# Attention in pairs of heads on row halves, with the probabilities scaled on GpSimd

## The chip, the cores and the metric

One core of a Trainium2 chip runs the whole program. The metric is the device time of one execution in microseconds; before, the median of three runs is 4497.36 us (4497.18 to 4500.56).

## The reference

The reference is a stack of six layers over 512 tokens of width 1024, all float32. The first two layers join two attentions each: A (8 heads, keys chosen by an indexer) and B (8 heads, a band of 128 keys and a sink logit), then C (8 heads; 31 compressed keys, and two causal branches, each with a gate) and D (8 latent heads of 64 + 32 dimensions). Then follow four layers with modulation by a conditioning vector: full attention over 512 tokens and 256 context tokens, attention with a neighbourhood bias (NA), a convolution and a Fourier mixer, each with an MLP. Every attention is a softmax of this kind:

```python
s = jnp.einsum('bqgrd,bnkgd->bngrqk', qb, kb).astype(jnp.float32) * scale
s = jnp.where(mask[None, :, None, None], s, -jnp.inf)
m = jnp.maximum(jnp.max(s, axis=-1, keepdims=True), sink)
p = jnp.exp(s - m)
p = p / (jnp.sum(p, axis=-1, keepdims=True) + jnp.exp(sink - m))
o = jnp.einsum('bngrqk,bnkgd->bnqgrd', p.astype(v.dtype), vb)
```

In C each branch's output is multiplied by its gate and the three are added; masked rows whose keys are all hidden give zero.

## The kernel before, in words

The program is written out by hand for each engine. A list of stages (project, norm, attention, compress, down, fast, rpb, conv and others) is built first, and each engine walks it with a function of the same name. At the end of a stage every engine waits for all others. Within a stage the order on each engine is what its loop emits, and semaphores are the only links.

Weights come through a ring of three slots (RING = 3). SP issues block b when block b - 3 is freed (L998), by PE's last matmul on it or by DVE's last sum. An ada block is a weight block that DVE multiplies by the conditioning vector and sums (L1868, L1872); PE reduces the sums over the partitions with small matmuls (`modulation`, L1064), DVE takes the result and starts on the next block. A block rides on a group of a project stage: `ride(a)` at the end of a group first does the modulation of the block before and then notes this one.

There are five attention stages: A and B together (8 passes), C (12), D (4), GQA (8 passes of 512 queries over 768 keys, then 8 of 256 context queries over 256) and NA (8 passes over 768 keys with a bias). A pass is two heads. Queries and keys of the two heads lie on partitions 0 to 63 and 64 to 127, except in D, where each head has 96 partitions of its own. The work is cut into units of 128 rows. In all but D a unit is 64 queries of both heads: POOL copies the two Q halves into the diagonal blocks of a 128x128 tile (L2318, L2319), whose other blocks are zero, and one matmul multiplies it by the keys of both heads. In D a unit is 128 queries of one head. For a unit u PE does, in this order,

```python
for u in range(U + lag + 4):
    if u < U:
        scores(u)
    if u >= lag + 4:
        weigh((u - lag - 4) // 4, (u - lag) % 4)
    if lag <= u < U + lag:
        turn(u - lag)
```

`scores` (L1283) also adds the mask as a bf16 matmul (L1287); `turn` (L1301) transposes the probabilities tile by tile; `weigh` (L1320) is a quarter of the weighting of four units (a chunk of 256 queries), on column halves, one for each head. DVE adds the bias in NA (L2059), takes the negated maximum (L2063, or L2066 and L2069 with a sink or a clamp), inverts the sum of the exponentials (L2085) and multiplies the probabilities by it and by the gate (L2089, L2091); ACT does the exponential with its sum (L1629) and copies the turned tiles from PSUM (L1612); DVE takes the output (L2101, L2103). Up to 512 keys four units are in flight (PSUM banks 0 to 3, turned tiles in banks 4 and 5, outputs in 6 and 7); at 768 keys there are two (two banks each, turned tiles in 4 and 5 as one). The bias of NA is a table in DRAM that POOL loads for each pass (L2226). f32 matmuls appear in the trace as two records each.

## Time and profile before

| | |
|---|---|
| median of three runs | 4497.36 us |
| profiled execution, its own time | 4497.19 us |
| its span | 4495.3 us |
| PE busy | 4225.3 us (94%) |
| DVE, ACT, POOL busy | 1807.4, 1002.6, 569.6 us |
| granted clock, mean | 0.951 |

The span runs from the first to the last instruction; the time has some 2 us around it. A busy time counts the records of an engine as one piece where they overlap; the ends of matmuls are modelled, and a record's end reaches some 0.17 us over the start of the next. A clock of 1.00 is 2.4 GHz.

### The profile page before, as it was taken

The page shows a single profiled execution, that of the slowest core. Times are in us where ns is not written, and L with a number is a line of the kernel's source. Part 1 is how long each engine was busy: PE and PEld are TensorE (multiplying, and loading weights), DVE is VectorE, ACT ScalarE, POOL GpSimd, SP SyncE. Part 2 cuts the span into 40 slices and gives each one's busy share as a digit, 9 for nine tenths or more (in the row PEclk, how much of TensorE's full clock was granted, in tenths as well). Part 3 has the DMA queues.
Part 4 walks back from the last instruction along what each step waited for, and adds up shares of the span by engine and source line. Part 5 has one row for each costly group of instructions (what it writes and reads, how often), then busy time and mean ns, then how long its engine had stood idle before and what let it go on. Part 6 is the DMA issues. An engine that isn't in the chain of part 4 may idle for free. (4 is left out here: it accounts for less than half of the span.)

```text
span 4495.3 us, 41307 instructions
## 1 busy us (share of the span) xinstructions
PE 4225.3 (94%) x15852; PEld 2623.4 (58%) x15856; DVE 1807.4 (40%) x3067; ACT 1002.6 (22%) x2179; POOL 569.6 (13%) x896
## 2 busy tenths in 40 slices
PE   8998979799999799999989999999999999999998
PEld 3354445244555356665545454888644788747887
DVE  3573347443266022112010384665264565404443
ACT  1150116232156121100010252201122202112020
POOL 0030013010012000000000121111130111101112
PEclk8999969689999799999999999999999999999999
DMA  3113320202000212232111101454210344211221
GB/s 131 60 38 107 120 69 11 76 1 87 26 17 1 54 56 94 94 112 94 56 56 56 51 23 38 143 176 150 75 56 19 119 162 169 80 52 66 88 94 38
DMA packets 206737, 339.16 MB, mean 75 GB/s; under 512 B 19472, under 2 KB 77232, under 8 KB 206512
## 3 DMA queue, kind: packets, MB, share of 16 engines
q1 hardware_dynamic: 188000, 320.42, 20.6%
q10 hardware_dynamic: 17136, 10.07, 0.9%
q0 software_dynamic: 1408, 6.03, 0.5%
q8 instruction: 129, 2.11, 0.2%
q14 instruction: 64, 0.52, 0.0%
HBM read 330.48 MB, written 6.03 MB: 75 GB/s over the span
## 5 line engine op out<-in xcount | busy, mean ns | idle before, releaser
L1096 PE MATMUL psum<-H,ring 128*128 128x512 f32 (+1 forms) x2608 | 1145.4, 599 | 33.5 <-issue 16.8
L1096 PEld LDWEIGHTS psum<-H,ring 128*128 128x128 f32 (+1 forms) x2608 | 494.9, 191 | 665.1 <-issue 651.7
L1224 PE MATMUL psum<-arena,ring 128*128 128x256 f32 x1536 | 343.3, 380 | 2.8 <-ACT arena L1512 2.8
L1283 PE MATMUL psum<-arena,sd 128*128 128x256 f32 (+4 forms) x896 | 311.1, 453 | 13.9 <-POOL sd L2319 10.5
L1872 DVE SCALAR_TENSOR_TENSOR arena<-ring,cond,arena 128x512 f32<-128x512 f32 x448 | 319.0, 750 | 8.0
L1224 PEld LDWEIGHTS psum<-arena,ring 128*128 128x128 f32 x1536 | 290.4, 190 | 44.0 <-ACT arena L1512 5.2
L2252 POOL TENSOR_TENSOR ring<-ring 128x1024 f32<-128x1024 f32 x48 | 162.4, 3383 | 813.1 <-DVE arena L1762 813.1
L1224 PE MATMUL psum<-arena 128*128 128x256 f32 x1152 | 255.5, 379 | 0.0
L2063 DVE TENSOR_REDUCE small<-psum 128x1 f32<-128x768 f32 (+4 forms) x288 | 198.5, 689 | 138.2 <-PE psum L1283 95.7
L1612 ACT ACTIVATE arena<-psum 128x768 f32<-128x768 f32 (+5 forms) x352 | 191.3, 543 | 221.2 <-PE psum L1301 217.8
L1224 PEld LDWEIGHTS psum<-arena 128*128 128x128 f32 x1152 | 218.9, 190 | 29.8
L1855 DVE TENSOR_TENSOR mods<-psum,vec 128x4 f32<-128x4 f32 (+1 forms) x48 | 7.7, 161 | 564.5 <-PE psum L1064 563.6
L1180 PE MATMUL psum<-arena,ring 128*128 128x512 f32 x512 | 225.4, 593 | 0.2 <-issue 0.2
L1629 ACT ACTIVATE arena<-psum,small 128x768 f32<-128x768 f32 (+5 forms) x352 | 219.1, 622 | 22.9 <-DVE small L2063 17.2
L1301 PE MATMUL psum<-ident,arena 128*128 128x128 f32 (+1 forms) x1240 | 210.7, 287 | 7.1 <-ACT arena L1612 3.2
L1096 PE MATMUL psum<-CH,ring 128*128 128x256 f32 x928 | 207.4, 382 | 0.0
L1301 PEld LDWEIGHTS psum<-ident,arena 128*128 128x128 f32 (+1 forms) x1240 | 133.5, 140 | 117.3 <-issue 79.3
L1320 PE MATMUL psum<-arena 128*64 128x256 f32 (+2 forms) x1360 | 192.5, 381 | 8.1 <-ACT arena L1612 7.1
L1283 PEld LDWEIGHTS psum<-arena,sd 128*128 128x128 f32 x896 | 151.0, 198 | 83.4 <-issue 75.1
L1096 PEld LDWEIGHTS psum<-CH,ring 128*128 128x128 f32 x928 | 176.6, 191 | 38.4 <-issue 12.1
L1224 PE MATMUL psum<-H,ring 128*128 128x256 f32 x768 | 183.5, 394 | 7.6 <-ACT H L1552 5.1
L1470 ACT ACTIVATE arena<-psum 128x512 f32<-128x512 f32 (+4 forms) x123 | 66.4, 541 | 549.8 <-PE psum L1096 549.5
(214 smaller groups left out, 4906.7 us busy)
## 6 DMA issues: line engine op xcount, KB each, us to landing
ring<-in_mlp_w SPq DMA_DIRECT2D x64, 2048.0 KB, 7.9
ring<-in_ada_w SPq DMA_DIRECT2D x48, 2048.0 KB, 7.9
ring<-in_na_qkv SPq DMA_DIRECT2D x6, 2048.0 KB, 7.9
ring<-in_pw SPq DMA_DIRECT2D x6, 2048.0 KB, 7.9
ring<-in_ab_in SPq DMA_DIRECT2D x5, 2048.0 KB, 7.8
ring<-in_cd_in SPq DMA_DIRECT2D x4, 2048.0 KB, 7.6
ring<-in_at_qkv SPq DMA_DIRECT2D x3, 2048.0 KB, 7.7
ring<-in_ab_out SPq DMA_DIRECT2D x2, 2048.0 KB, 11.0
```

The source lines that it names most:

```text
L1096: last = nc.tensor.matmul(out, lhs, rhs, start=(k == 0), stop=(k == len(t.pairs) - 1))
L1180: last = nc.tensor.matmul(bank(m), w[:, k, P * m:P * m + P], hid[:, KD * kb + k, :], start=(kb == 0 and k == 0), stop=(kb == 3 and k == KD ...
L1224: last = nc.tensor.matmul(out, w[:, i, P * m:P * m + P], x[:, i, :], start=(opens and m == 0 and i == 0), stop=(i == k - 1), skip_group_ch ...
L1283: last = nc.tensor.matmul(psum[:, buf + c0:buf + c1], q, p["k"](head, a * P + c0, a * P + c1), start=True, stop=not masks)
L1301: last = nc.tensor.transpose(psum[0:w, t0 + j * P:t0 + j * P + P], probs[u % d["nb"]][:, j * P:j * P + w], ident[:, :])
L1320: last = nc.tensor.matmul(psum[HD * g:HD * g + HD, (6 + pr % 2) * BANK + q0:(6 + pr % 2) * BANK + q1], p["v"](g, kt), turned_b[0:p["krows" ...
L1470: nc.scalar.activation(t.dst, src, ACT.Copy).then_inc(act_took, 1)
L1612: nc.scalar.activation(dst, src, ACT.Copy).then_inc(copied, 1)
L1629: nc.scalar.activation(probs[u % d["nb"]][:, 0:nk], psum[:, s0:s0 + nk], ACT.Exp, bias=small[:, c:c + 1], accum_out=small[:, 8 + c:9 + c]) ...
L1872: ins = nc.vector.scalar_tensor_tensor(partial[:, v, :], w[:, k, :], cond[:, k, v:v + 1], partial[:, v, :], ALU.mult, ALU.add)
L2063: nc.vector.tensor_reduce(small[:, c:c + 1], psum[:, s0:s0 + nk], AX, ALU.max, negate=True).then_inc(negmax_ready, 1)
L2252: nc.gpsimd.tensor_tensor(a21, a11, a21, ALU.subtract).then_inc(s3_made, 1)
```

## The change

- A unit becomes a pair: 128 queries of two heads. Each head's scores are a matmul of its own on 64 rows, partitions 0 to 63 or 64 to 127 (`of_head`); the diagonal tile, its copies on POOL and half_select are gone. D keeps 96 rows.
- Two pairs are in flight in every stage. At 768 keys a pair takes three banks, and its second head's columns start with key tiles 4 and 5 so that no matmul crosses a bank. The fourth matmul of a pair waits for the second through half_scored, since the two share a bank. The turned tiles and the outputs share banks 6 and 7, and each waits until what was in the bank is taken. Four tiles of one head are turned and copied at a time; the third group of a pair (tiles 4 and 5 of both heads) is copied by DVE.
- The multiplication by the inverse sum and the gate moves from DVE to POOL.
- The sink, and the clamp of the compressed branch (as a key of -1e29), become one more column of the scores by a matmul with the identity (L1346 of the new program); DVE's and ACT's operations for them go. The compression stage no longer moves the gates.
- NA's bias lies in CX and CH, once for each head, and is loaded for both row halves of a tile: four transfers a pass instead of two.
- An ada block moves: it no longer rides on the group at c0 == 2048 of the first layer's projection, and a group with no weights and this block stands after the second group of the second layer's. All later blocks shift in the ring.
- The sinks are loaded in four parts.

```diff
@@ first layer's projection
-            ab_groups.append((b, ab_tiles(b, c0, c0 + 512), next_ada() if c0 == 2048 else None))
+            ab_groups.append((b, ab_tiles(b, c0, c0 + 512), None))
@@ second layer's projection
             groups_.append((b, (c0, c1), next_ada()))
+            if c0 == 512:
+                groups_.append((None, None, next_ada()))
@@ the order of the pairs
+        def order(st):
+            pairs, chunks = st["pairs"], st["chunks"]
+            for i in range(len(pairs) + 6):
+                if i < len(pairs):
+                    yield "scores", pairs[i], None
+                if 0 <= i - 2 < len(pairs):
+                    for t in pairs[i - 2]["turns"]:
+                        yield "turn", t, pairs[i - 2]
+                if st["wide"]:
+                    if i >= 5 and i % 2 and (i - 5) // 2 < len(chunks):
+                        yield "weigh", chunks[(i - 5) // 2], None
+                elif i >= 4 and (i - 4) // 2 < len(chunks):
+                    yield "weigh", chunks[(i - 4) // 2], i % 2
@@ PE
+                    for b in pair["banks"]:
+                        open_bank(b)
+                    runs = [(0, 0, BANK), (1, BANK, nk), (1, 0, BANK), (0, BANK, nk)] if nk > BANK else [(0, 0, nk), (1, 0, nk)]
+                    for m, (g, k0, k1) in enumerate(runs):
+                        at = off[g] + pair["column"](g, k0 // P)
+                        if m == 3:
+                            n["half"] += 1
+                            pe.wait_ge(half_scored, n["half"])
+                        last = nc.tensor.matmul(psum[:, at:at + k1 - k0], p["q"](g, qt * P, qt * P + P),
+                                                p["k"](g, a * P + k0, a * P + k1), start=(m < 3), stop=not masks,
+                                                skip_group_check=nk > BANK or p["sink"] is not None)
+                        if m == 1 and nk > BANK:
+                            last.then_inc(half_scored, 1)
...
+                        if p["sink"] is not None:
+                            last = nc.tensor.matmul(psum[:, off[g] + nk:off[g] + nk + 1], ident[:, :], p["sink"](g),
+                                                    start=False, stop=True, skip_group_check=True)
...
+                    for b in pair["banks"]:
+                        bank_freed[b] = (exp_done, 2 * pair["id"] + 2)
+                def turn(t, pair):
+                    rows, c0 = min(P, pair["p"]["krows"]), t["bank"] * BANK
+                    pe.wait_ge(probs_ready, 2 * pair["id"] + t["gs"][-1] + 1)
+                    open_bank(t["bank"])
@@ ACT
+                for i in range(len(pairs) + 2):
+                    if st["wide"] and i >= 2:
+                        copies(pairs[i - 2], i - 2)
+                    if i < len(pairs):
+                        exponential(pairs[i], i, 0)
+                        exponential(pairs[i], i, 1)
+                    if not st["wide"] and i >= 2:
+                        copies(pairs[i - 2], i - 2)
@@ DVE
+                for i in range(len(pairs) + 8):
+                    if i < len(pairs):
+                        negmax(pairs[i], 0)
+                        negmax(pairs[i], 1)
+                    if 0 <= i - 1 < len(pairs):
+                        scale(pairs[i - 1], 0)
+                        scale(pairs[i - 1], 1)
+                    if 0 <= i - 2 < len(pairs):
+                        copies(pairs[i - 2], i - 2)
+                    j = i - (5 if st["wide"] else 6)
+                    if j >= 0 and j % 2 == 0 and j // 2 < len(chunks):
+                        take(chunks[j // 2])
@@ POOL
-                        nc.gpsimd.tensor_copy(q_diagonal[0:HD, u % Q_BUFS, 0:HD], q[0:HD]).then_inc(pool_steps, 1)
-                        nc.gpsimd.tensor_copy(q_diagonal[HD:P, u % Q_BUFS, HD:P], q[HD:P]).then_inc(q_ready, 1)
+                            pool.wait_ge(inverse_ready, u + 1)
+                            pb, by = pair["probs"][g][:, 0:nk], small[:, 24 + c:25 + c]
+                            if p["gate"] is not None:
+                                nc.gpsimd.tensor_scalar(pb, pb, by, p["gate"](pair["qt"], g), ALU.mult,
+                                                        ALU.mult).then_inc(probs_ready, 1)
+                            else:
+                                nc.gpsimd.tensor_scalar(pb, pb, by, None, ALU.mult).then_inc(probs_ready, 1)
```

The order of the instructions in two places. PE in the GQA stage at 768 keys, before (L1301 transposes, L1283 scores, L1320 weighting; two units):

```order
L1301 MATMUL psum<-ident,arena 128x128 x6
L1283 MATMUL psum<-arena,sd 128x512
L1283 MATMUL psum<-arena,sd 128x256
L1320 MATMUL psum<-arena 64x256 x2
L1301 MATMUL psum<-ident,arena 128x128 x6
L1283 MATMUL psum<-arena,sd 128x512
L1283 MATMUL psum<-arena,sd 128x256
L1320 MATMUL psum<-arena 64x256 x4
```

and in the change (L1335 scores, L1360 transposes, L1381 weighting; two pairs):

```order
L1335 MATMUL psum<-arena 128x512
L1335 MATMUL psum<-arena 128x256
L1335 MATMUL psum<-arena 128x512
L1335 MATMUL psum<-arena 128x256
L1360 MATMUL psum<-ident,arena 128x128 x12
L1335 MATMUL psum<-arena 128x512
L1335 MATMUL psum<-arena 128x256
L1335 MATMUL psum<-arena 128x512
L1335 MATMUL psum<-arena 128x256
L1360 MATMUL psum<-ident,arena 128x128 x12
L1381 MATMUL psum<-arena 64x256 x12
```

The weighting of a chunk stood in quarters between scores and transposes and now stands in one piece behind the transposes of every second pair. PE in the second layer's projection, before (L1096 a group of 32 matmuls, L1064 a modulation):

```order
L1096 MATMUL psum<-H,ring 128x512 x32
L1064 MATMUL psum<-ones,arena 128x1 x8
L1096 MATMUL psum<-H,ring 128x512 x32
L1064 MATMUL psum<-ones,arena 128x1 x8
L1096 MATMUL psum<-H,ring 128x512 x32
```

and in the change (L1155 a group, L1123 a modulation):

```order
L1155 MATMUL psum<-H,ring 128x512 x32
L1123 MATMUL psum<-ones,arena 128x1 x8
L1155 MATMUL psum<-H,ring 128x512 x32
L1123 MATMUL psum<-ones,arena 128x1 x16
L1155 MATMUL psum<-H,ring 128x512 x32
```

Two modulations stand behind one another after the second group; the one after the first output block of the first layer is gone.

## Rows read from the trace of the kernel before

**Rows 1.** Attention stages: window, length, PE, PEld, DVE, ACT, POOL busy, clock, DMA
```profile
251.00:339.00 88.00, 83.17 (x556) 49.41 (x560) 70.06 (x264) 61.98 (x226) 31.32 (x127) 1.00 0.13 48
666.00:781.00 115.00, 110.36 (x700) 64.84 (x702) 90.79 (x355) 77.59 (x288) 47.21 (x189) 0.94 0.01 1
932.00:980.00 48.00, 45.79 (x262) 25.68 (x264) 33.00 (x100) 31.95 (x98) 0.00 (x0) 0.92 0.00 1
1236.00:1465.00 229.00, 224.14 (x1217) 123.10 (x1216) 141.29 (x304) 135.47 (x289) 42.87 (x185) 1.00 0.03 9
2538.00:2732.00 194.00, 189.46 (x1024) 106.95 (x1024) 153.62 (x263) 108.66 (x192) 35.61 (x138) 0.98 0.10 26
```

**Rows 2.** Timeline at 768 keys: start, us, engine, line, operation, count [idle before]
```profile
1300.62 0.87 PE L1301 MATMUL psum<-ident,arena 128*128 128x128 f32 x6
...
1301.33 1.46 PE L1283 MATMUL psum<-arena,sd 128*128 128x512 f32 x4
1301.53 0.81 ACT L1612 ACTIVATE arena<-psum 128x768 f32<-128x768 f32 x1 [0.99 <-PE psum L1301]
...
1302.72 1.08 PE L1320 MATMUL psum<-arena 128*64 128x256 f32 x8
1302.83 0.96 DVE L2063 TENSOR_REDUCE small<-psum 128x1 f32<-128x768 f32 x1 [0.40 <-PE psum L1283]
...
1303.70 0.15 DVE L2085 RECIPROCAL small<-small 128x1 f32<-128x1 f32 x1
...
1303.74 0.87 PE L1301 MATMUL psum<-ident,arena 128*128 128x128 f32 x6
...
1306.42 0.87 PE L1301 MATMUL psum<-ident,arena 128*128 128x128 f32 x6
```

**Rows 3.** Timeline of the context passes, 256 keys
```profile
1440.99 0.44 PE L1301 MATMUL psum<-ident,arena 128*128 128x128 f32 x2
...
1443.57 0.44 PE L1301 MATMUL psum<-ident,arena 128*128 128x128 f32 x2
```

**Rows 4.** Timeline of the last attention, 768 keys with a bias
```profile
2621.85 0.70 DVE L2059 TENSOR_TENSOR psum<-psum,CX 128x512 f32<-128x512 f32 x1 [0.70 <-PE psum L1283]
...
2622.33 0.87 PE L1301 MATMUL psum<-ident,arena 128*128 128x128 f32 x6
2622.59 0.96 DVE L2063 TENSOR_REDUCE small<-psum 128x1 f32<-128x768 f32 x1
...
2628.12 0.87 PE L1301 MATMUL psum<-ident,arena 128*128 128x128 f32 x6
```

**Rows 5.** Timeline of PE at the indexer's matmuls on row halves
```profile
115.11 1.13 PE L1158 MATMUL psum<-arena 64*128 64x512 f32 x4
116.17 1.04 PE L1121 MATMUL psum<-arena 128*22 128x512 f32 x2
```

**Rows 6.** POOL's groups by line and shape: count, busy us, mean ns, idle before
```profile
L2318 POOL COPY sd<-arena 64x64 f32<-64x64 f32 x320 | 75.5, 236 | 395.1 <-PE psum L1283 301.2 <-PE psum L1287 86.2 <-remote 4.5
...
L2269 POOL TENSOR_TENSOR arena<-arena 128x512 f32<-128x512 f32 x24 | 30.5, 1269 | 70.2 <-DVE arena L1825 70.2
...
L2269 POOL TENSOR_TENSOR arena<-arena 128x256 f32<-128x256 f32 x24 | 17.4, 723 | 120.1 <-DVE arena L1825 120.1
```

**Rows 7.** Timelines of PE and DVE in the second layer's projection
```profile
412.95 29.86 PE L1096 MATMUL psum<-H,ring 128*128 128x512 f32 x64 [0.93 <-DVE H L1964]
...
471.91 1.84 PE L1064 MATMUL psum<-ones,arena 128*128 128x1 f32 x16
473.61 27.71 PE L1096 MATMUL psum<-H,ring 128*128 128x512 f32 x64
...
474.67 9.36 DVE L1872 SCALAR_TENSOR_TENSOR arena<-ring,cond,arena 128x512 f32<-128x512 f32 x14
```

**Rows 8.** Group of ACT's copies of 512 turned columns
```profile
L1612 ACT ACTIVATE arena<-psum 128x512 f32<-128x512 f32 x32 | 19.1, 597 | 7.1 <-PE psum L1301 6.9
```

**Rows 9.** Transfers of the page: count, KB each, us to landing
```profile
ring<-in_cd_in SPq DMA_DIRECT2D x4, 2048.0 KB, 7.6
```

More of the change, by code:

```diff
@@ new lines, in weigh @@
+                def weigh(chunk, half):
+                    p, c0, parts, n_parts = chunk["p"], chunk["c0"], chunk["parts"], len(chunk["parts"])
+                    if half != 1:
+                        pe.wait_ge(act_copied, chunk["copied"][0])
+                        if chunk["copied"][1]:
+                            pe.wait_ge(dve_copied, chunk["copied"][1])
+                        if st["wide"] or (p["first"] and c0 == 0):
+                            open_bank(chunk["bank"])
+                    starts = st["wide"] or (c0 == 0 and p["first"])
+                    ends = st["wide"] or p["last"]
+                    split = n_parts if half is None else n_parts // 4 * 2
+                    for i in range(split if half == 1 else 0, n_parts if half == 1 else split):
@@ L1325, in weigh @@
-                    if quarter == 3:
-                        last.then_inc(pv_done, 1)
-                        if p["last"] and j + 4 == p["units"]:
-                            pairs[0] += 1
-                U, lag = len(units), d["turn"]
-                for u in range(U + lag + 4):
-                    if u < U:
-                        scores(u)
-                    if u >= lag + 4:
-                        weigh((u - lag - 4) // 4, (u - lag) % 4)
-                    if lag <= u < U + lag:
-                        turn(u - lag)
@@ L1338, in attention @@
-                n["unit"] += U
-                n["pair"] += pairs[0]
+                            psum[HD * g:HD * g + HD, at + q0:at + q1], p["v"](g, kt),
+                            chunk["turned"][0:p["krows"], kt, g, q0 - c0:q1 - c0], start=(i < 2 and starts),
+                            stop=(i >= n_parts - 2 and ends), skip_group_check=True)
+                    if half != 0:
+                        last.then_inc(pv_done, 1)
+                        if chunk["takes"]:
+                            bank_freed[chunk["bank"]] = (o_taken, chunk["taken"])
@@ L1341, in compress @@
+                for kind, x, y in order(st):
+                    if kind == "scores":
+                        scores(x)
+                    elif kind == "turn":
+                        turn(x, y)
+                    else:
+                        weigh(x, y)
             def compress(st):
@@ L1369, in compress @@
                     last.then_inc(misc_pe, 1)
[L1370 to L1376 removed]
+                n["misc"] += 6
             def latnorm(st):
@@ L1631, in attention, with exponential @@
-                n["unit"] += U
-                n["pv"] += U // 4
-                act.wait_ge(copied, n["unit"])
+                pairs = st["pairs"]
+                def exponential(pair, i, g):
+                    p, nk, off = pair["p"], pair["nk"], pair["off"][g]
+                    u = 2 * pair["id"] + g
+                    c = u % 8
+                    act.wait_ge(negmax_ready, 2 * pair["id"] + 2 if nk > BANK else u + 1)
+                    if i >= 2:
+                        before = [t["seq"] for t in pairs[i - 2]["turns"] if g in t["gs"]]
+                        act.wait_ge(turned, before[-1])
+                    more = p["sink"] is not None
+                    nc.scalar.activation(pair["probs"][g][:, 0:nk + more], psum[:, off:off + nk + more], ACT.Exp,
+                                         bias=small[:, c:c + 1], accum_out=small[:, 8 + c:9 + c]).then_inc(exp_done, 1)
@@ L1635, in compress @@
+                act.wait_ge(act_copied, pairs[-1]["copied"][0])
             def compress(st):
@@ L2122, in compress @@
+                dve.wait_ge(o_taken, chunks[-1]["taken"])
             def compress(st):
```

451 lines of the change are left out of this document (189 added, 262 removed).

## The prediction

> **What bounds the kernel now.** I read the page first (one core, PE busy 94% of the span, clock 0.951), then asked for the busy time of each engine in the five attention stages [rows 1]. See two things there: the stages last 88, 115, 48, 229 and 194 us, 674 of 4495 us in all, and PE is busy in 94 to 98% of each, while DVE stands at 62 to 80%, ACT at 56 to 70% and POOL at 41% at most. So PE's own list of instructions sets these stages, and the question is what the change leaves on that list and what it makes PE wait for. The timeline of the 768-key stage [rows 2] gives prices. Six transposes start at 1300.62 and the scores at 1301.33; the scores (512 and 256 keys, two records each) take the 1.39 us to 1302.72; units follow each other after 3.12 and 2.68 us in turn, and differ by four passes of the weighting, so one pass is 0.107 us. Two units (128 queries of two heads) take 5.80 us. Streaming is 1.29 + 0.64 + 0.64 = 2.57 us a unit, so changing between the three kinds of matmul costs 0.33 us a unit.
>
> **1. Row halves for the scores.** Before, a block-diagonal Q multiplies 128 rows; after, each head multiplies on its own 64 rows. The work in keys is the same (two heads by 128 queries, nk keys each), so this pays only if the two halves run at once. The trace has such a pair: the indexer's 64-row matmuls of two heads [rows 5] start together, and 512 keys of both take 1.06 us until the next matmul, with four passes. One after another they would be 4 x 0.433 = 1.73 us (64 passes of 512 columns take 27.71 us [rows 7]); at once 2 x 0.433 plus 0.2 of fixed cost is 1.07. I take full overlap: 1.39 us for a pair of heads at 768 keys instead of 2.78. The third matmul of a pair (keys 0 to 511 of the second head) has a bank of its own; the fourth waits for the second (the counter half_scored), whose data are long there when the first ends.
>
> **2. The 768-key steps.** PE's list per pair is now scores 1.39, transposes 12 x 0.107 and a half of 24 weighting passes: 3.96 us plus changes, against 5.80. It will not get there. The turned tiles and the weighted sums share banks 6 and 7, so the third group of transposes waits until ACT has copied the first: handover 0.27 (1301.26 to 1301.53 [rows 2]), copy of 512 columns 0.60 [rows 8], 0.2 back to PE (my allowance for a semaphore to PE, here and below): 1.07 us after the first group, where it could start after 0.43. The weighting waits for the second copy, 0.5 later. With 0.15 to change to transposes (1303.58 to 1303.74), even steps: 1.39 + 0.15 + 0.43 + 1.07 + 0.43 = 3.47; odd steps 1.39 + 0.15 + 0.43 + 0.27 + 1.10 + 0.20 + 2.65 = 6.19; floor 9.66 us for two pairs (11.60 before).
> The second limit is the new hop. The order is fixed: scores of the next pair, then both maxima on DVE, then the reciprocals of this pair, two multiplications on POOL, this pair's transposes, copy, weighting. Around two steps: 1.39 + 0.21 (1302.62 to 1302.83) + 0.87 + 0.96 for two maxima [rows 2] + 0.15 + 2p + 0.20 + 0.43 + 0.27 + 0.60 + 0.20 + 2.65 = 7.93 + 2p, with p the time of one 128x768 multiplication on POOL. In the last attention each maximum has a bias addition ahead of it, 0.74 from start to start [rows 4], so 9.41 + 2p.
>
> **The price p.** POOL has no such operation in this trace. The nearest from below is its one-input copy, 0.236 for 64 elements; from above its two-input multiplication, 1.269 for 512 and 0.723 for 256 [rows 6], that is 0.18 fixed and 2.13 ns an element. With the same fixed part the copy gives 0.8 ns an element: p between 0.80 and 1.82. The operation reads one tensor and two scalars, so I stay near the copy: p = 0.95. Then two pairs take 9.83 in the first 768-key stage and 11.31 in the last, against 11.60.
> The Trainium skill (GPSIMD Engine Reference, Engine selection) says that one-input work on GpSimd is "roughly line-rate"; by that p would be 0.8 and the total 4428. The same page (Elementwise, side-by-side cycle accounting) gives 1.8 cycles an element as the best case of a tight loop; by that p would be near 1.3 and the total 4462. No row here shows either.
>
> **3. The sum.**
> - GQA stage, 32 pairs at 768 keys: 16 x (11.60 - 9.83) = -28. Its 16 context pairs take 2.58 each now [rows 3]; scores halve (-0.43) and a set of changes goes; with POOL in the loop I take -0.5 each, -8. Together -36.
> - NA stage: 16 x (11.60 - 11.31) = -5, and +1 for the first bias, which DVE already waits for, since it is now eight transfers instead of four: -4.
> - A and B (88 us): 256 keys save 0.43, so 4 x 1280 keys save 8.5 and 4 x 896 save 6.0; a set of changes fewer, 32 x 0.25 = 8; the sink is now a matmul by the identity, four passes a pair at the 0.106 of the ada block's small matmuls (16 in 1.70 us [rows 7]), 16 x 0.43 = 6.8 back. That is -16; the loop of two pairs will not keep all of it: -12.
> - C (115 us): 8 x 1280 keys, 17; changes 12; the same extra column for the 31-key passes, +7: -20, as above with a little held back.
> - D (48 us): 96 rows, no halves; fewer changes (-4), later probabilities (+1.5): -2.5.
> - The moved ada block. It leaves the end of the first projection, where DVE's sums lie under PE's value tiles, and comes as a group of its own without weights after the second group of the second layer. PE there does the modulation matmuls twice in a row, and the second needs the DVE sums of the block before, which start only after the first. Where one block rides now, the group ends at 471.91, the modulation takes 1.70 and DVE's sums end at 484.03, 12.1 after the group [rows 7]; with 0.2 and another modulation the next weights start 14.0 us after the group's end instead of 1.7, +12.3, less 1.7 for the one no longer done after the first output block: +10.6. The clock follows: behind the wait for the norm the 64 passes of 412.95 took 29.86 us, those of 473.61 27.71 [rows 7], +2.2. The next weights also find their ring slot free only at the group's end; the 7.6 us of loading [rows 9] lie under the DVE sums. In all +13.
> - Inputs: three more small transfers ahead of the first weights, +1; the gate matmuls and copy of the compression gone, -1. POOL's copies of Q, 320 for each half [rows 6], go at no gain: it idled and PE seldom waited for them.
> Sum: -36 - 4 - 12 - 20 - 2.5 + 13 = -61.5. Against the profiled execution's 4497.2 (median 4497.4) this is **4436 us**.
>
> **The rivals.**
> *Halves in lock step* (0.14). In-order starts could make the four matmuls of a pair run as two rounds of 512 columns: 1.72 us instead of 1.29. The equal pair of rows 5 can't tell. PE's floor becomes 10.52 for two pairs, and the NA loop 11.74: 11 us and 7 us less gain, 4454.
> *A loop price in between* (0.19), p = 1.3: each loop grows by 0.7 for two pairs, 11 us in each 768-key stage, and a little in the others: about 4462.
> *POOL at the two-input rate, slower than before* (0.10), p = 1.82. The GQA period is 11.57, so the stage keeps only its context gain (-5); NA's is 13.05, +23 +1; POOL also delays the short stages, where I leave -5, -12 and +1; with +13 for the ada block the sum is +16: 4513. It decides from p = 1.1 on in NA alone (9.41 + 2p = 11.6) and from about 1.7 on for the whole. For it: two-input multiplications are the only arithmetic POOL does here, at that rate. Against it: the copy.
> *It pays for itself only* (0.05): the pairs are not in flight as described, since banks or buffers are held longer than the order shows, PE waits away what the halves save, and the time stays within 9 us.
> A lower clock I hold for unlikely: PE would stream 70% of the time in NA and its gaps stay near 1 us; it held full clock at two gaps per 2.9 us.
>
> **How the numbers follow.** A difference under 0.2% (9 us) could not be told from none. Forecast 0.52, lock step 0.14, middle price 0.19: faster 0.85; same 0.05; slower 0.10. The range takes p = 0.80 (4428, and up to 20 below for the short stages keeping all and the ada stall being half) and reaches above over both faster rivals together (4480): 4405 to 4480.
>
> **What would show it.** POOL's TENSOR_SCALAR at 128x768 near 0.95 us; two score rows of a pair starting together, 1.4 us per pair; PE waiting for ACT copies and for POOL in transposes; PE idle of about 12 us once after the second group of the second layer, for DVE; stages of about 76, 95, 45, 193 and 190 us. A POOL row over 1.7 us, or scores of 2.8 us, would make the forecast wrong.

## The result, and the profile after

The changed kernel takes 4628.85 us (median of four runs, 4627.25 to 4635.16), the kernel before 4498.48 on the same chip: a ratio of 1.0293, 95% interval 1.0277 to 1.0309. It is 130 us **slower**, where 61 us faster was forecast, and outside the range. The profiled execution of the changed kernel took 4627.25 us (span 4625.5, mean granted clock 0.932; before 0.951).

The busy time in the five attention stages of the changed kernel, as [rows 1] show it before (window, length, PE, PEld, DVE, ACT, POOL busy, clock, DMA; each window runs from the first score matmul to just behind the last weighting matmul):

```profile
249.40:341.90 92.50, 78.86 (x624) 47.27 (x624) 34.12 (x136) 52.69 (x170) 60.73 (x64) 1.00 0.07 24
681.50:795.00 113.50, 105.20 (x768) 60.99 (x768) 41.34 (x196) 72.82 (x258) 50.19 (x96) 0.93 0.01 2
946.20:1006.00 59.80, 50.05 (x272) 29.58 (x272) 18.47 (x68) 30.43 (x90) 34.16 (x32) 0.90 0.00 1
1260.00:1523.00 263.00, 209.40 (x1216) 129.05 (x1216) 109.69 (x248) 121.86 (x274) 168.84 (x96) 0.90 0.04 11
2592.00:2857.00 265.00, 193.30 (x1024) 120.42 (x1024) 133.30 (x240) 98.23 (x194) 156.70 (x96) 0.81 0.15 38
```

Windows cut in this way are 87.4, 115.9, 48.4, 228.9 and 195.0 us long before, so the stages together went from 675.6 to 793.8 us. That is 118 of the 130 us, and 104 of them are in the two 768-key stages (the fourth and fifth rows). There PE is no longer busy all the time (80% and 73%, before 98% and 97%), and its clock is 0.90 and 0.81 instead of 1.00 and 0.98. No engine took PE's place: POOL is busy for 64% and 59%.

POOL's groups for the new multiplication (line, operation, shapes, count, busy us, mean ns, idle before):

```profile
L2352 POOL TENSOR_SCALAR arena<-arena,small 128x768 f32<-128x768 f32 x112 | 245.3, 2203 | 198.0 <-DVE small L2108 197.9
...
L2352 POOL TENSOR_SCALAR arena<-arena,small 128x512 f32<-128x512 f32 x16 | 24.8, 1563 | 0.0
...
L2352 POOL TENSOR_SCALAR arena<-arena,small 128x128 f32<-128x128 f32 x24 | 14.2, 601 | 34.0 <-DVE small L2108 33.9
L2349 POOL TENSOR_SCALAR arena<-arena,small 128x512 f32<-128x512 f32 x16 | 12.2, 770 | 1.9 <-DVE small L2108 1.9
...
L2349 POOL TENSOR_SCALAR arena<-arena,small 128x128 f32<-128x128 f32 x16 | 7.0, 448 | 9.8 <-DVE small L2108 9.8
```

L2352 multiplies by one scalar column, L2349 by two (the inverse sum and the gate). One operation costs 2.50 ns an element ((2203 - 601) / 640) and 0.28 us fixed; two operations in one instruction cost a third of that, 0.84 ns an element. The time of one 128x768 multiplication, the prediction's p, was 2.20 us, above its upper bound of 1.82.

Two rows of the list of PE's waits (us in total, times, longest), and PE's, POOL's and the weight loads' (PEld) timelines over two pairs of the first 768-key stage, which [rows 2] show before (sd_rstd is one of the tiles that hold probabilities; the last row of PE's timeline is cut by the end of the window asked for):

```profile
PE psum L1360 <- POOL arena L2352: 95.9, 96, 2.0
...
PE psum L1360 <- POOL sd_rstd L2352: 21.6, 15, 1.5
```

```profile
1329.86 1.89 PE L1335 MATMUL psum<-arena 64*128 64x512 f32 x8
1331.69 1.09 PE L1360 MATMUL psum<-ident,arena 128*128 128x128 f32 x8
...
1333.68 1.89 PE L1335 MATMUL psum<-arena 64*128 64x512 f32 x8
1336.04 0.66 PE L1360 MATMUL psum<-ident,arena 128*128 128x128 f32 x4 [0.47 <-POOL arena L2352]
1338.22 1.74 PE L1360 MATMUL psum<-ident,arena 128*128 128x128 f32 x8 [1.52 <-POOL arena L2352]
1339.89 3.79 PE L1381 MATMUL psum<-arena 128*64 128x256 f32 x24
1343.61 0.70 PE L1335 MATMUL psum<-arena 64*128 64x512 f32 x3
```

```profile
1333.78 8.74 POOL L2352 TENSOR_SCALAR arena<-arena,small 128x768 f32<-128x768 f32 x4 [5.01 <-DVE small L2108]
```

```profile
1329.86 0.73 PEld L1335 LDWEIGHTS psum<-arena 64*128 64x128 f32 x6 [0.39 <-issue]
1331.06 0.29 PEld L1335 LDWEIGHTS psum<-arena 64*128 64x128 f32 x2 [0.47 <-PE psum L1335]
```

Two stretches of the same two pairs in the columns of the stages above; the granted clock stands behind POOL's busy time:

```profile
1338.22:1339.89 1.67, 1.67 (x8) 1.34 (x8) 0.00 (x0) 0.60 (x1) 1.67 (x1) 0.58 0.00 0
1339.89:1341.50 1.61, 1.61 (x9) 1.01 (x10) 0.69 (x1) 1.44 (x3) 1.61 (x2) 0.50 0.00 0
```

See four things. The period of two pairs is 13.75 us (1329.86 to 1343.61), 11.60 before. The transposes of the odd pair wait for POOL, head by head. The scores of a pair take 1.83 us (1329.86 to 1331.69), not 1.39, and the weight loads of the fourth matmul wait for L1335, another matmul of the same pair: that is the counter half_scored. And behind the waits for POOL (0.47 and 1.52 us) the weighting's 24 passes take 3.72 us (1339.89 to 1343.61), where 2.57 was reckoned: the granted clock was 0.58 in the transposes just ahead of them and 0.50, the lower of its two levels (1.2 GHz), in the first 1.61 us of them.

### The profile page after: what moved, and what is told of

It reads as the page before. It is cut to its first block and busy times, and to the rows that moved or that the text cites. A ratio compares the mean times of both kernels' runs of the same rounds, so it can differ in the third digit from the quotient of the medians.

```text
span 4625.5 us, 40970 instructions
## 1 busy us (share of the span) xinstructions
PE 4214.6 (91%) x15976; PEld 2643.9 (57%) x15976; DVE 1655.2 (36%) x2668; ACT 957.0 (21%) x2062; POOL 875.9 (19%) x616
## 5 line engine op out<-in xcount | busy, mean ns | idle before, releaser
L1155 PE MATMUL psum<-H,ring 128*128 128x512 f32 (+1 forms) x2608 | 1151.5, 601 | 33.0 <-issue 16.6
L1155 PEld LDWEIGHTS psum<-H,ring 128*128 128x128 f32 (+1 forms) x2608 | 497.4, 192 | 669.0 <-issue 656.2
L2352 POOL TENSOR_SCALAR arena<-arena,small 128x768 f32<-128x768 f32 (+3 forms) x240 | 369.1, 1552 | 287.1 <-DVE small L2108 286.9
L1283 PE MATMUL psum<-arena,ring 128*128 128x256 f32 x1536 | 343.3, 380 | 2.8 <-ACT arena L1563 2.8
L1283 PEld LDWEIGHTS psum<-arena,ring 128*128 128x128 f32 x1536 | 290.4, 190 | 44.0 <-ACT arena L1563 5.2
L1360 PE MATMUL psum<-ident,arena 128*128 128x128 f32 (+1 forms) x1144 | 197.9, 304 | 114.4 <-POOL arena L2352 95.9
L2098 DVE TENSOR_REDUCE small<-psum 128x1 f32<-128x768 f32 (+7 forms) x352 | 204.0, 614 | 226.6 <-PE psum L1342 110.8
L1283 PE MATMUL psum<-arena 128*128 128x256 f32 x1152 | 255.5, 379 | 0.0
L1335 PE MATMUL psum<-arena 64*128 64x512 f32 (+4 forms) x960 | 220.2, 501 | 21.4 <-ACT arena L1654 17.0
L1283 PEld LDWEIGHTS psum<-arena 128*128 128x128 f32 x1152 | 218.9, 190 | 29.8
L1654 ACT ACTIVATE arena<-psum,small 128x768 f32<-128x768 f32 (+7 forms) x336 | 204.4, 613 | 151.5 <-DVE small L2098 90.7
L1360 PEld LDWEIGHTS psum<-ident,arena 128*128 128x128 f32 (+1 forms) x1144 | 135.3, 152 | 169.9 <-POOL arena L2352 127.9
L1155 PE MATMUL psum<-CH,ring 128*128 128x256 f32 x928 | 207.6, 382 | 0.0
L2329 POOL TENSOR_TENSOR arena<-arena 128x512 f32<-128x512 f32 (+2 forms) x46 | 56.5, 1234 | 770.4 <-DVE arena L2031 763.6
L1155 PEld LDWEIGHTS psum<-CH,ring 128*128 128x128 f32 x928 | 176.7, 191 | 38.3 <-issue 12.0
L1666 ACT ACTIVATE arena<-psum 128x512 f32<-128x512 f32 (+3 forms) x272 | 144.2, 553 | 249.5 <-PE psum L1360 249.1
L1381 PE MATMUL psum<-arena 128*64 128x256 f32 (+2 forms) x1360 | 193.9, 426 | 1.9 <-ACT arena L1666 1.7
L1283 PE MATMUL psum<-H,ring 128*128 128x256 f32 x768 | 182.5, 393 | 7.6 <-ACT H L1603 5.1
```

Source lines behind the costliest of these rows:

```text
L1155: last = nc.tensor.matmul(out, lhs, rhs, start=(k == 0), stop=(k == len(t.pairs) - 1))
L1283: last = nc.tensor.matmul(out, w[:, i, P * m:P * m + P], x[:, i, :], start=(opens and m == 0 and i == 0), stop=(i == k - 1), skip_group_ch ...
L1335: last = nc.tensor.matmul(psum[:, at:at + k1 - k0], p["q"](g, qt * P, qt * P + P), p["k"](g, a * P + k0, a * P + k1), start=(m < 3), stop= ...
L1360: last = nc.tensor.transpose(psum[0:rows, c0:c0 + P], pair["probs"][g][:, k0:k0 + rows], ident[:, :])
L1381: last = nc.tensor.matmul(psum[HD * g:HD * g + HD, at + q0:at + q1], p["v"](g, kt), chunk["turned"][0:p["krows"], kt, g, q0 - c0:q1 - c0], ...
L1654: nc.scalar.activation(pair["probs"][g][:, 0:nk + more], psum[:, off:off + nk + more], ACT.Exp, bias=small[:, c:c + 1], accum_out=small[:, ...
```

## The experiments

Twelve kernels were run, all of them the changed kernel with edits. The ratios are to the kernel before, whose median was 4497.3 to 4498.2 us beside them. A difference between two changed versions is the difference of their medians.

**The price.** A second scalar makes POOL run the form of L2349.

```diff
-                                nc.gpsimd.tensor_scalar(pb, pb, by, None, ALU.mult).then_inc(probs_ready, 1)
+                                nc.gpsimd.tensor_scalar(pb, pb, by, ones[:, :], ALU.mult,
+                                                        ALU.mult).then_inc(probs_ready, 1)
```

> The changed kernel with one edit: the multiplication without a gate gets a second scalar, a column of ones, so that POOL runs the form which takes two scalars. Theory (the price is that of the one-scalar form, not of the operation): a 128x768 multiplication falls from 2.20 us to about 0.99 (the gated ones took 0.34 us + 0.84 ns an element), two pairs at 768 keys from 13.7 us to 10.3 to 10.8, the last attention from about 13.8 to 11.8, and the time from 4629 to 4460 to 4530 us. Rival (POOL is slow at this because it shares its way to the tiles with VectorE, or because of the length): the multiplication stays above 2 us and the time above 4600.

Measured: 4481.15 us, ratio to before 0.9963 [0.9948, 0.9978], that is 148 us less than the changed kernel by one operand and one operation more. POOL's groups, then PE's timeline over two pairs:

```profile
L2352 POOL TENSOR_SCALAR arena<-arena,small,ones 128x768 f32<-128x768 f32 x112 | 109.0, 981 | 237.1 <-DVE small L2108 237.0
...
L2352 POOL TENSOR_SCALAR arena<-arena,small,ones 128x512 f32<-128x512 f32 x16 | 12.1, 768 | 0.1
```

```profile
1289.84 1.89 PE L1335 MATMUL psum<-arena 64*128 64x512 f32 x8
1291.67 1.09 PE L1360 MATMUL psum<-ident,arena 128*128 128x128 f32 x8
...
1297.47 2.81 PE L1381 MATMUL psum<-arena 128*64 128x256 f32 x24
1300.21 1.89 PE L1335 MATMUL psum<-arena 64*128 64x512 f32 x8
```

The period is 10.37 us, no wait for POOL is left in the pairs of 768 keys, and the weighting takes 2.74 us again. The stage's context pairs of 256 keys keep eight waits for POOL, 7.5 us together. So the loss is the price of the form, and the lower clock came with the waits. The time lies in the range that was expected (4460 to 4530), and the rival of a price that stays is out. Three of its stages (the gated one and the two at 768 keys), in the windows' columns as above; the other two last 80.7 and 50.2 us:

```profile
...
669.50:783.20 113.70, 105.30 (x768) 61.08 (x768) 41.41 (x196) 72.91 (x258) 50.19 (x96) 0.93 0.01 2
...
1233.70:1440.00 206.30, 184.90 (x1217) 114.83 (x1218) 109.72 (x248) 120.54 (x274) 79.60 (x96) 0.99 0.05 14
2508.40:2708.00 199.60, 160.66 (x1024) 104.39 (x1024) 131.70 (x240) 98.11 (x194) 78.78 (x96) 0.96 0.20 51
```

**Which form is dear.** The second scalar as a constant:

```diff
-                                nc.gpsimd.tensor_scalar(pb, pb, by, None, ALU.mult).then_inc(probs_ready, 1)
+                                nc.gpsimd.tensor_scalar(pb, pb, by, 1.0, ALU.mult, ALU.mult).then_inc(probs_ready, 1)
```

> The multiplication without a gate as one scalar column and a second multiplication by the constant 1.0. Theory (the dear form is the one with a single operation): 128x768 near 0.98 us, as with the column of ones. Rival (the cheap form needs two scalar columns): 2.2 us and a time near 4629.

Measured once: 4485.69 us, and the multiplication a little cheaper still. One execution can't rank it against the column of ones (4481.15).

```profile
L2352 POOL TENSOR_SCALAR arena<-arena,small 128x768 f32<-128x768 f32 x112 | 100.1, 904 | 243.7 <-DVE small L2108 243.3
```

A price list. This kernel leaves out the division by the sum in the passes without a gate:

```diff
-                                nc.gpsimd.tensor_scalar(pb, pb, by, None, ALU.mult).then_inc(probs_ready, 1)
+                                if g == 0:
+                                    nc.gpsimd.tensor_scalar(pb, pb, 1.0, None, ALU.mult).then_inc(probs_ready, 1)
+                                else:
+                                    nc.gpsimd.tensor_copy(pb, pb).then_inc(probs_ready, 1)
```

> Only a price list: the changed kernel where the multiplication without a gate is left out, and in its place POOL multiplies the first head by the constant 1.0 (one operation, no scalar column) and copies the second head onto itself. It leaves the division by the sum out of those passes. Theory (one operation alone is the dear form, whatever the scalar is): first head near 2.1 us at 128x768, the copy near the 0.8 that was the lower bound of the forecast. Rival (the dear form is one operation by a column): first head 0.9 or less, time below 4490.

```profile
L2353 POOL TENSOR_SCALAR arena<-arena 128x768 f32<-128x768 f32 x64 | 136.4, 2131 | 215.7 <-DVE small L2108 215.6
...
L2355 POOL COPY arena<-arena 128x768 f32<-128x768 f32 x48 | 39.6, 825 | 0.0
```

A single operation is dear with a constant too; the scalar column is not the reason. The copy takes 0.825 us, so the lower bound of 0.80 was close for a copy, and the operation as it was written was simply not of that kind. One execution took 4519.66 us.

**Does the price add along the loop?** The second scalar for the second head of a pair alone:

```diff
-                                nc.gpsimd.tensor_scalar(pb, pb, by, None, ALU.mult).then_inc(probs_ready, 1)
+                                nc.gpsimd.tensor_scalar(pb, pb, by, None if g == 0 else ones[:, :], ALU.mult,
+                                                        *(() if g == 0 else (ALU.mult,))).then_inc(probs_ready, 1)
```

> The changed kernel with the second scalar for the second head of a pair alone: one multiplication at 2.20 us, one at 0.98. Theory (price adds along the loop): 7.93 + 0.43 + 3.2 = 11.55 us for two pairs in the first 768-key stage, plus a little clock, 13.0 in the last; time 4525 to 4555, between 4629 and 4481. Rival (only the slower of the two counts): above 4590.

Measured: 4540.43 us, ratio 1.0093 [1.0078, 1.0108], between the two versions. PE's timeline:

```profile
1296.21 1.89 PE L1335 MATMUL psum<-arena 64*128 64x512 f32 x8
1298.56 0.66 PE L1360 MATMUL psum<-ident,arena 128*128 128x128 f32 x4 [0.46 <-POOL arena L2352]
1299.53 1.09 PE L1360 MATMUL psum<-ident,arena 128*128 128x128 f32 x8 [0.31 <-POOL arena L2352]
1300.96 2.81 PE L1381 MATMUL psum<-arena 128*64 128x256 f32 x24 [0.34 <-ACT arena L1666]
...
1307.52 1.89 PE L1335 MATMUL psum<-arena 64*128 64x512 f32 x8
```

Two pairs take 11.31 us (1296.21 to 1307.52), 11.55 expected. So both heads' prices count, and the rival (only the slower of the two, above 4590 us) is out.

**Is it the loop?** Here the dear form stays. At 768 keys (`wide`) the reciprocals, which release POOL, move between the two maxima of the next pair:

```diff
                     if i < len(pairs):
                         negmax(pairs[i], 0)
-                        negmax(pairs[i], 1)
+                        if not st["wide"]:
+                            negmax(pairs[i], 1)
                     if 0 <= i - 1 < len(pairs):
                         scale(pairs[i - 1], 0)
                         scale(pairs[i - 1], 1)
+                    if i < len(pairs) and st["wide"]:
+                        negmax(pairs[i], 1)
```

> The changed kernel itself, with its dear one-scalar form; only the reciprocals go between the two maxima of the next pair at 768 keys. Theory (the loop of two pairs through VectorE and POOL sets the period, its terms add): 0.9 us less for two pairs in the first 768-key stage and 1.6 us in the last, 40 us in all: 4590. Rival (POOL's own throughput or PE's clock sets it): 4620 to 4629.

Measured: 4569.53 us, ratio 1.0157 [1.014, 1.0174], 59 us less than the changed kernel at an unchanged price of POOL.

```profile
1297.99 1.89 PE L1335 MATMUL psum<-arena 64*128 64x512 f32 x8
...
1305.48 1.09 PE L1360 MATMUL psum<-ident,arena 128*128 128x128 f32 x8 [1.20 <-POOL arena L2355]
1306.91 2.81 PE L1381 MATMUL psum<-arena 128*64 128x256 f32 x24 [0.34 <-ACT arena L1666]
1309.65 1.68 PE L1335 MATMUL psum<-arena 64*128 64x512 f32 x7
```

The period fell by 2.1 us (13.75 to 11.66), more than the 0.9 that the move takes out of the loop. Of the rest 0.98 is the weighting, back from 3.72 to 2.74 us (1306.91 to 1309.65), and 0.24 the eight transposes ahead of it, from 1.67 to 1.43 (1305.48 to 1306.91): less wait also gave the clock back (0.98 in this stage, 0.90 in the changed kernel). So the loop sets the period, not POOL's throughput, which is the same in both. The 59 us are more than the 40 expected, which counted no clock.

**The multiplication elsewhere.** Back on VectorE behind the reciprocals, pairs kept; POOL's loop over the heads is empty:

```diff
-                    nc.vector.reciprocal(small[:, 24 + c:25 + c], small[:, 8 + c:9 + c]).then_inc(inverse_ready, 1)
+                    last = nc.vector.reciprocal(small[:, 24 + c:25 + c], small[:, 8 + c:9 + c])
...
+                        nc.vector.tensor_scalar(pb, pb, by, None, ALU.mult).then_inc(probs_ready, 1)
...
-                        for g in range(2):
+                        for g in ():
```

> The changed kernel with the multiplications back on VectorE behind the reciprocals, pairs and order kept. Theory (the wait for POOL is the loss, the pairs are a gain): 0.62 us a multiplication at 768 keys as before, period of two pairs near PE's floor with halves in lock step, 10.0 to 10.5 us, time 4450 to 4510, at most 20 us from the two-scalar version. Rival (the pairs themselves lose: banks held too long, or VectorE becomes the bound): above 4560.

Measured: 4472.30 us, ratio 0.9942 [0.9927, 0.9957], 9 us less than the two-scalar version, with the same periods: 10.37 us, and 11.57 in the last attention. So the pairs themselves are a gain, and the rival that they lose (above 4560) is out. Then one head on each engine (two scalars on POOL, a counter of its own for VectorE's heads):

```diff
-                    pe.wait_ge(probs_ready, 2 * pair["id"] + t["gs"][-1] + 1)
+                    for g in t["gs"]:
+                        pe.wait_ge((probs_ready, probs_dve)[g], pair["id"] + 1)
```

> Two-scalar form on POOL for the first head of a pair, VectorE multiplies the second head, so the two lie beside each other. The loop of two pairs becomes 7.93 + 0.43 + 1.0 = 9.4 us, below PE's own list, so both 768-key stages go to the floor of PE (10.1 to 10.5 us): 5 to 25 us less than the two-scalar version. Rival (the loop does not bound once the price is small): equal to it within 3 us.

Measured: 4473.68 us, ratio 0.9946 [0.9931, 0.9961]: 7 us less, which is the lower end of what was expected. The last attention did not move (11.56): POOL's half grew dearer beside VectorE's, and PE waits 1.12 us for it in every two pairs there. POOL's and VectorE's timelines in the first 768-key stage:

```profile
1294.59 1.39 POOL L2364 TENSOR_SCALAR arena<-arena,small,ones 128x768 f32<-128x768 f32 x1 [5.17 <-DVE small L2109]
```

```profile
1294.59 0.62 DVE L2120 TENSOR_SCALAR arena<-arena,small 128x768 f32<-128x768 f32 x1
```

**The ada block.**

```diff
-            ab_groups.append((b, ab_tiles(b, c0, c0 + 512), None))
+            ab_groups.append((b, ab_tiles(b, c0, c0 + 512), next_ada() if c0 == 2048 else None))
...
-            if c0 == 512:
-                groups_.append((None, None, next_ada()))
```

> Two-scalar version, and the moved ada block put back to the last output block of the first projection. Theory: 13 to 15 us less than the two-scalar version (two stalls of DVE sums less, one modulation more). Rival (the stall only moves, or the block costs as much in its old place): within 3 us of it.

Measured: 4468.81 us, ratio 0.9935 [0.9918, 0.9951], 12.3 us less than the two-scalar version (13 to 15 expected). PE's timeline of the changed kernel shows where they were (before: the 1.84 at 471.91 of [rows 7]):

```profile
474.14 1.84 PE L1123 MATMUL psum<-ones,arena 128*128 128x1 f32 x16
486.32 3.58 PE L1123 MATMUL psum<-ones,arena 128*128 128x1 f32 x16 [10.33 <-DVE arena L1909]
489.75 30.52 PE L1155 MATMUL psum<-H,ring 128*128 128x512 f32 x64
```

From the group's end to the next weights it is 15.6 us (474.14 to 489.75; 14.0 was reckoned), and the 64 passes behind take 2.8 us longer than the 27.71 of [rows 7]. With the one modulation that is saved elsewhere this is more than 12.3, so the block is not free in its old place either; how much it costs there was not taken apart.

**The halves.** In the gated stage of the two-scalar version both heads at 512 keys take 1.06 us until the next matmul (2 x 0.43 and 0.2 of fixed time), so two matmuls of equal length overlap fully:

```profile
694.03 1.13 PE L1335 MATMUL psum<-arena 64*128 64x512 f32 x4
695.09 0.29 PE L1342 MATMUL psum<-diagm,identb 128*128 128x128 bf16 x2
```

At 768 keys a 512 stands beside a 256. Two scalars, and six matmuls of 256 keys:

```diff
-                    runs = [(0, 0, BANK), (1, BANK, nk), (1, 0, BANK), (0, BANK, nk)] if nk > BANK else [(0, 0, nk), (1, 0, nk)]
+                    runs = [(0, 0, 256), (1, BANK, nk), (0, 256, BANK), (1, 0, 256), (0, BANK, nk),
+                            (1, 256, BANK)] if nk > BANK else [(0, 0, nk), (1, 0, nk)]
...
-                        if m == 3:
+                        if m == 4:
```

> Two-scalar version, and the scores of a pair at 768 keys cut into six matmuls of 256 keys, head by head in turn, so that the halves always hold equal lengths. In the two-scalar version 256, 384 and 512 keys of both heads take 0.64, 0.85 and 1.07 us (full overlap and 0.21 fixed), 768 keys in unequal lengths 1.83. Theory (only unequal neighbours keep the halves in step): 3 x 0.427 + 0.2 = 1.5 us a pair, two pairs 10.37 to 9.7 us in the first 768-key stage and 11.57 to 10.9 in the last, 22 us less than the two-scalar version. Rival (weight loads of the halves come one after another, 12 loads of 0.186 us): 2.0 us or more a pair, and 5 to 20 us slower than it.

Measured: 4464.38 us, ratio 0.9927 [0.991, 0.9943], 17 us less than the two-scalar version. PE's timeline and that of the weight loads:

```profile
1286.11 1.57 PE L1336 MATMUL psum<-arena 64*128 64x256 f32 x12
1287.61 1.09 PE L1361 MATMUL psum<-ident,arena 128*128 128x128 f32 x8
```

```profile
1286.11 1.16 PEld L1336 LDWEIGHTS psum<-arena 64*128 64x128 f32 x12 [0.39 <-issue]
```

The same keys now take 1.50 us (1286.11 to 1287.61), so the rival (12 loads one after another, 2.0 us) is out. But the edit changes two things, the lengths and the place of the wait on half_scored, which now stands ahead of the fifth matmul. The loads say which one the time went to. In the changed kernel the six loads of the first three matmuls are through 0.73 us after the pair's start (1329.86), and the two of the fourth begin only at 1331.06, 1.20 us after it, released by the second matmul (0.47 before in PEld's row). Here the twelve loads have no such gap. The unequal lengths themselves overlap: in the two-scalar version, whose pairs also take 1.83 us, two records of 512 columns start together 0.54 us after a pair's start (1289.84), the first matmul's second one and the third matmul's first (one short stretch; count, ns, first and last start):

```profile
L1335 PE MATMUL psum<-arena x2: 589/589/589, 1290.4 to 1290.4; 64*128 64x512 f32 x2
```

By the lengths the first head's half is free 0.96 us after the start (2 x 0.43 and 0.1, half of the fixed time, to start; an estimate), so the wait costs 0.24 us; with 0.1 to start again that turns 1.50 into 1.84, against 1.83 measured. It is released only after the first matmul's data are through too, though the second is half as long. No run has the unequal lengths without this wait, so the division of the 0.33 us rests on these rows.

In the last attention only 0.3 of the 0.66 us for two pairs came through (period 11.25): there PE waits for POOL that much longer (1.06 and 0.32 us, before 0.72 and 0.31).

**The last attention's loop.** Two scalars, and the reciprocals between the maxima by the same edit as above:

> Two-scalar version; on VectorE at 768 keys the reciprocals of a pair go between the two maxima of the next pair instead of behind both, so POOL starts one maximum (with its bias addition: 1.6 us) earlier. Theory (in the last attention the loop through VectorE's maxima and POOL sets the period, in the first 768-key stage PE's own list does): last attention 11.57 to about 10.4 us for two pairs, first stage unchanged at 10.37; 15 to 20 us less than the two-scalar version. Rival (VectorE's maxima or ACT's exponentials bound the last attention): within 3 us of it.

Measured: 4475.36 us, ratio 0.9947 [0.9933, 0.9962], 6 us less than the two-scalar version, where 15 to 20 were expected; its own four runs spread over 11 us (4470 to 4481). PE's timeline of the last attention:

```profile
2578.94 0.60 PE L1360 MATMUL psum<-ident,sd_rstd 128*128 128x128 f32 x4
2580.69 0.41 PE L1360 MATMUL psum<-ident,arena 128*128 128x128 f32 x2 [1.15 <-ACT arena L1666]
```

POOL is in time now, and ACT is late next: it runs the next pair's two exponentials (2578.18 to 2579.95) ahead of the copies. The period is 11.19 us, from 11.57, where 10.4 was expected: the theory missed the size, and the rival (under 3 us, VectorE or ACT the bound) had named ACT but not the gain.

**Together.** Two scalars, equal halves, reciprocals between the maxima, ada block back:

> Two scalars, equal halves, reciprocals between the maxima, and the ada block put back. If the three gains add: 4481 - 22 - 18 - 12 = 4429 us; if the loop binds again once PE's list is shorter, 4430 to 4445.

Measured: 4450.69 us, ratio 0.9887 [0.987, 0.9903], with runs from 4438 to 4453. Both expectations missed (4429 if the gains add, else 4430 to 4445): together the parts give 30 us over the two-scalar version, one by one 17, 6 and 12. Then with the constant 1.0 as second factor, and VectorE multiplying in the stages of at most 512 keys:

> All three edits of e8 with the constant 1.0 as second factor, and in the attentions of at most 512 keys the multiplications back on VectorE. Theory: the short stages lose PE's waits for POOL (5 us) and the clock falls less often in the gated one (up to 9 us): 4430 to 4445 us against 4451. Rival (POOL's waits cost nothing there, VectorE's extra work does): 4450 to 4460.

Measured: 4440.49 us, ratio 0.987 [0.9855, 0.9885]: 57 us under the kernel before, 188 under the changed one, and inside what was expected (4430 to 4445). The 10 us to the version before are of two edits at once and less than that one's own spread of 15, so neither edit's share is shown. Two pairs take 9.72 us in the first 768-key stage.

```profile
1300.35 1.57 PE L1334 MATMUL psum<-arena 64*128 64x256 f32 x12
...
1310.07 1.13 PE L1334 MATMUL psum<-arena 64*128 64x256 f32 x8
```

## Why the prediction was wrong

**The price p** is the step that failed. The prediction took 0.95 us because "the operation reads one tensor and two scalars"; L2352, the line that sets both 768-key stages, takes one scalar and one operation, and that form took 2.20. The two-scalar form takes 0.98, so 0.95 was the price of another line. The upper bound failed with it: the two-input multiplication at 2.13 ns an element was taken for the dearest thing POOL does, and the one-operation form takes 2.50. POOL had never run that form in the trace, and a bound from other operations needs a reason that it holds.
The Trainium skill (GPSIMD Engine Reference, Elementwise, side-by-side cycle accounting) reckons 512 elements of its best loop at 768 ns; the two-scalar rows agree (768 and 770 ns), the one-scalar row does not (1563). Its "roughly line-rate" for one input (Engine selection) held for the copy (825 ns at 768) and not for the one-operation multiplication.

**The loop** was right. With 0.43 more for the scores, 7.93 + 0.43 + 2 x 2.20 = 12.76 us, and 0.98 of slower weighting and 0.24 of slower transposes make 13.98, against 13.75 measured: its terms are some 0.2 too large together. In the last attention 9.41 + 0.43 + 4.40 = 14.24, against 15.11 (two pairs at 2701.00) at a clock of 0.81 in the stage; with two scalars 11.80 reckoned, 11.57 measured. The earlier reciprocals and the single dear head confirm it from both sides. The rival "POOL at the two-input rate, slower than before" had the mechanism and the sign; its 4513 was too low since p passed even its price, and since it counted no loss of clock and no dearer scores.

**A lower clock I hold for unlikely** was wrong: with two waits for POOL in every two pairs (0.47 and 1.52 us, in the last attention 1.93 and 1.52) the stages stood at 0.90 and 0.81; without these waits, or with a single one of 1.20, the first of them was at 0.99 and 0.98. It cost about 20 us in the first 768-key stage (1.22, the slower weighting and transposes, in each of 16 periods).

**Row halves.** Two equal matmuls overlap fully (1.06 us for 512 keys). At 768 keys a pair took 1.83 us instead of 1.39, and the step that failed is "the fourth waits for the second (the counter half_scored), whose data are long there when the first ends": the fourth's loads were held until 1.20 us after the pair's start. The rival of the lock step, at 0.14, came near that size (1.72, and some 0.1 for changing), but by luck: it wants two rounds of 512 columns, and the third matmul starts 0.54 us after the first, beside the first's second half, where a first round would take 0.86. The six equal matmuls, where nothing waits, bring 1.50; the 0.11 over 1.39 is the rest of the fixed time (the prediction had 0.2 in its 1.07 for 512 keys, and 0.1 in its 1.39).
The Trainium skill (TensorEngine Tiling (Array Packing), Key Properties) says that tiles operate independently; the 1.06 us for two matmuls of 512 keys agrees, and the 1.83 beside 1.50 for the same keys shows that a wait from one tile to the other takes some of it back.

**The sum, term by term** (forecast; changed kernel; two-scalar version, in us against before, stages by their windows): first 768-key stage -36; +34; -23. Last attention -4; +70; +5. A and B -12; +5; -7. C -20; -2; -2. D -2.5; +11; +2. The ada block +13, measured 12.3. In the two-scalar version the price was the forecast's own, and 16 us of the 61 were left (its terms here add to 13). So even at the forecast's price three quarters of the gain are missing:

- The first 768-key stage, 13 us: 16 x 0.54 = 9 by the periods 10.37 and 9.83, which are the dearer scores; 2 in the context pairs, which save 0.37 us each instead of 0.5 with POOL in their loop; 2 not taken apart.
- The last attention, 9 us: 4 by the period (11.57 for 11.31), and the first bias, put at +1. It is there 12.5 us after the last matmul of the projection ahead, 9.6 before, so +2.9. The window shows more, since it starts at the first score: PE waited 4.38 us for POOL's copies of Q there, and waits 0.80 now. These 3.6 us are also the difference between 13 and 16.
- The short stages, 18 us in C, 5 in A and B, 4 in D. The 0.2 us of fixed time of every score pair, seen in [rows 5], was left out: at 128 keys a pair takes 0.42 us, two units took 2 x 0.22, so nothing is saved. Over the 32 masked pairs of A and B, and as many in C, this is about 7 us each. In C 5 us more are PE's waits for POOL's gated multiplication. D has no halves. How the rest of C's and D's expected gain divides between sinks, changes of kind and waits was not taken apart.

## What to carry to other kernels

Price an operation by a row with the same opcode and the same number of operations and scalars in it; if the trace has none, time that form by itself before building a pipeline on it. On POOL, write a one-scalar multiplication with a second factor of 1.0 (tried here in f32, with 128 to 768 elements in a row). When a new engine is put between two others, add its time to the loop of buffers and maxima that closes over it, count the clock that PE loses while it waits, and look for what is queued in front of the next instruction once that wait is gone. A counter between two matmuls is a wait like any other: the timeline of the weight loads shows it where PE's own timeline shows no gap.

## What the runs showed that was not expected

- POOL's tensor-scalar multiplication of 128x768: one operation 2203 ns (2131 with a constant), two operations 981 (904 with the second factor a constant). More work in the instruction takes less than half the time.
- POOL and VectorE multiplying at once: POOL's 0.98 us became 1.39 while VectorE's stayed at 0.62; both started at 1294.59. The Trainium skill (SBUF — State Buffer, Who interferes with whom) says that the two share a port pair, that some modes of VectorE, which `tensor_scalar` can enter, use it, and that whoever issues first then has it for the whole instruction. The 0.41 us more on POOL, within VectorE's 0.62, are compatible with that; which mode VectorE ran in, no run shows.
- The wait on half_scored was released only 1.20 us after a pair's start, though the second matmul, which it waits for, is half as long as the first: the signal of the shorter matmul came after the longer one in front of it was through.
- The gated stage's clock differs between nearly equal kernels: it was 0.93 in the two-scalar version and 0.83 with the reciprocals moved at 768 keys, which changes nothing in that stage, and its length 113.7 and 122.2 us. The four runs of the latter kernel lay between 4470 and 4481 us at mean clocks of 0.948 to 0.944; in which stage they differ, no profile shows. Versions within 10 us of each other can't be ranked by one profile; what sets this clock stays open.
